# Pre-made weight sums for the second feed-forward of a two-block transformer kernel

## The reference

```python
def conv_ffn(x, w_up, conv_w, conv_b, w_down):      # w_up [1024, 5632], w_down [2816, 1024]
    h = x @ w_up
    h = causal depthwise convolution of width 3 over tokens, per column of h, + conv_b
    a, g = jnp.split(h, 2, axis=-1)
    return (jax.nn.silu(g) * a) @ w_down
```

## Time and profile before

| | before |
|---|---|
| median of 3 runs | 3193.47 us (3189.94 to 3194.23) |
| span of the profiled execution | 3197.4 us, 3.9 us above the median |
| PE busy | 3000.9 us, 94% |
| DVE, ACT, POOL busy | 1954.1, 1224.8, 606.6 us |
| loop of E, from first to last product | 1245.2 to 1657 us |
| loop of H, from first to last product | 2484.3 to 2929 us |

### The profile page before, as it was taken

How to read it: one execution, slowest core, us unless ns; L and a number is a source line. 1 busy time by engine, 2 the same in 40 slices (tenths; PEclk the granted TensorE clock), 3 DMA queues, 4 the chain that set the end, 5 groups by cost and what they waited for, 6 DMA issues and landing times.

```text
span 3197.4 us, 40840 instructions
## 1 busy us (share of the span) xinstructions
PE 3000.9 (94%) x15215; PEld 2446.6 (77%) x15215; DVE 1954.1 (61%) x2600; ACT 1224.8 (38%) x1900; POOL 606.6 (19%) x533
## 2 busy tenths in 40 slices
PE   8999999999989898999999988999888899999997
PEld 7777878878867677888878877888777677777886
DVE  3555565674674547555556674555646777776667
ACT  3531541531632445333322133565734443333212
POOL 3210110210221301322210000333411222221000
PEclk8999999999989899999999999999989999999999
DMA  4232212212222542222232244343334122223233
GB/s 138 69 94 59 89 60 67 94 54 73 82 80 77 213 145 86 79 79 79 79 113 105 93 131 123 86 135 122 120 106 146 53 79 79 79 72 105 93 105 119
DMA packets 227118, 308.16 MB, mean 96 GB/s; under 512 B 12162, under 2 KB 175248, under 8 KB 224416
## 3 DMA queue, kind: packets, MB, share of 16 engines
q1 hardware_dynamic: 207648, 244.93, 24.1%
q0 software_dynamic: 13520, 44.48, 4.1%
q10 hardware_dynamic: 5808, 16.79, 1.9%
HBM read 223.26 MB, written 82.90 MB: 96 GB/s over the span
## 4 chain that ended last, share of the span: by engine, by line
PE 66%; issue 12%; DVE 9%; ACT 4%; DMA 4%; POOL 4%; SPq 0%; POOLq 0%; ACTq 0%; DVEq 0%
PE PS L658 20%; PE PS L364 19%; PE PS L2314 13%; PE PS L1442 2%; PE PS L1408 1%; PE PS L1336 1%; POOL down_raw L1979 1%; POOL down_raw L1982 1%; PE PS L1325 1%; PE PS L2919 1%; DMA sb_branch<-u_scratch 1%; POOL down_raw L1977 1%; PE PS L2906 1%; DVE hL L439 1%; PE PS L1501 1%
## 5 line engine op out<-in xcount | busy, mean ns | idle before, releaser
L658 PE MATMUL PS<-hH,w_H 128*128 128x512 f32 x1072 | 455.8, 425 | 28.2 <-DVE w_L L321 15.3
L658 PE MATMUL PS<-hH,w_L 128*128 128x512 f32 x1072 | 428.2, 399 | 0.0
L658 PE MATMUL PS<-hL,w_H 128*128 128x512 f32 x1072 | 425.9, 397 | 0.0
L2133 DVE TENSOR_TENSOR ffn_sum<-ffn_sum,PS 128x1024 f32<-128x1024 f32 x160 | 195.4, 1221 | 139.4 <-PE PS L364 139.4
L321 DVE TENSOR_TENSOR w_L<-w_raw,w_H 128x1024 fp32r<-128x1024 f32 x107 | 133.6, 1251 | 217.4 <-ACT w_H L316 217.4
L658 PEld LDWEIGHTS PS<-hH,w_H 128*128 128x128 f32 x1072 | 208.0, 194 | 74.0 <-issue 16.0
L658 PEld LDWEIGHTS PS<-hH,w_L 128*128 128x128 f32 x1072 | 205.8, 192 | 46.8
L2314 PE MATMUL PS<-hH,fast_w 128*128 128x512 f32 x672 | 227.2, 399 | 10.3 <-ACT gate_up L2068 7.6
L658 PEld LDWEIGHTS PS<-hL,w_H 128*128 128x128 f32 x1072 | 207.7, 194 | 35.9 <-issue 1.7
L2212 DVE TENSOR_TENSOR gate_up<-PS,gate_up 128x512 f32<-128x512 f32 x210 | 144.1, 686 | 133.8 <-PE PS L2314 128.7
L2314 PE MATMUL PS<-sums,w_H 128*128 128x512 f32 x672 | 213.9, 400 | 9.3 <-DVE gate_up L2212 8.8
(11 more groups left out here) (459 smaller groups left out, 6569.1 us busy)
## 6 DMA issues: line engine op xcount, KB each, us to landing
w_raw<-in_w_in SPq DMA_DIRECT2D x62, 512.0 KB, 4.4
u_scratch<-unit_staged SPq DMA_DIRECT2D x50, 512.5 KB, 4.9
w_raw<-in_w_up SPq DMA_DIRECT2D x44, 512.0 KB, 4.2
hidden_scratch<-hidden SPq DMA_DIRECT2D x42, 512.0 KB, 3.0
gate_up<-hidden_scratch SPq DMA_DIRECT2D x20, 1024.0 KB, 4.9
w_raw<-in_w_ffn_gate SPq DMA_DIRECT2D x22, 512.0 KB, 3.9
w_raw<-in_w_ffn_up SPq DMA_DIRECT2D x22, 512.0 KB, 5.2
u_scratch<-unit_staged_f SPq DMA_DIRECT2D x21, 512.0 KB, 4.3
```

The costliest lines, as they stand in the source:

```text
L658: mm = e.matmul(PS[:, f.bank(o, half), :], w[:, k0 + k, :], x[:, k, half * HALF:(half + 1) * HALF], start=(k == 0 and j == 0), stop=(k == ...
L2133: e.tensor_tensor(yacc[:, b, :], yacc[:, b, :], bank2(4 + 2 * (b % 2)), ALU.add).then_inc(added, 1)
```

## The change

The four weight sums of H are no longer made tile by tile on GpSimd. All of T1 to T4, for all tiles, is made once in DRAM, in two tensors `up2_sums` of [1024 x 2816] float32, by 32 DMAs that GpSimd issues in stage B: 16 plain copies and 16 that add to their destination. Each moves 128 rows of 2816 numbers (1.44 MB), and each but the first waits for the completion of the one before. They are issued 2 + 4 + 4 in each of the first three pairs and 2 in the last. In H, SP loads for each tile the gate tile (512 KB), the half of the up tile that is still used raw (256 KB) and both sum tiles (512 KB each). GpSimd has nothing to do in H's loop. A DMA can add but not subtract, so all sums T become additions, and the signs move to the token sums and to `tile_sum`; E keeps GpSimd's sums, as additions. P6 goes to a PSUM bank of its own (3). In both E and H, tile 1's load moves behind the wait for the end of the stage before (`ffn_memory_free`).

```diff
+        up2_sums = [nc.dram_tensor(f"up2_sums{i}", [D, DFF], F32, kind="Internal").ap() for i in range(2)]
-            e.tensor_tensor(s1, s1, x2, ALU.add).then_inc(s, 1)
+            e.tensor_tensor(s1, s1, x2, ALU.subtract).then_inc(s, 1)
...
+        def up2_sum_parts(e):
+            w = a["w_up_2"][0]
+            gate, up = w[:, DFF:2 * DFF], w[:, 0:DFF]
+            top, low = slice(0, HALF), slice(HALF, D)
+            steps = [((0, top), gate[top], False), ((1, top), up[top], False),
+                     ((0, top), up[top], True), ((1, top), up[low], True),
+                     ((0, low), (0, top), False), ((0, low), up[low], True),
+                     ((1, low), (0, low), False), ((1, low), gate[low], True)]
+            n = 0
+            for (i, rows), src, add in steps:
+                dst = up2_sums[i][rows]
+                src = up2_sums[src[0]][src[1]] if isinstance(src, tuple) else src
+                for part in range(4):
+                    blk = slice(part * P, (part + 1) * P)
+                    if n:
+                        e.wait_ge(sem("up2_summed"), 16 * n)
+                    e.dma_start(dst[blk], src[blk], accum_op=ALU.add if add else ALU.bypass,
+                                max_dma_last_dim=2 * DFF)\
+                        .then_inc(sem("up2_summed"), 16)
+                    n += 1
+                    yield
...
         def pool_B(e):
+            parts = up2_sum_parts(e)
             for p in range(NPAIR):
...
                 if p == LAST:
                     o_low(range(4))
+                else:
+                    sums(2)
                 e.wait_ge(sem("rw_prepared"), at(PREP_OF["all"], p, 6))
...
                     e.memset(t[:, :, :], 0.0).then_inc(sem("inverse_zeroed"), 1)
+                sums(2 if p == LAST else 4)
                 for q in range(4):
...
+                sums(4)
                 e.wait_ge(sem("o_rw_written"), p + 1)
                 e.dma_start(o_scr[p + NPAIR], o_rw[:, :]).then_inc(sem("o_rw_stored"), 16)
...
-        Q_BANK, Q_FIRST = (0, 1, 0, 1, 2, 1, 2), (0, 1, 4)
+        Q_BANK, Q_FIRST = (0, 1, 0, 1, 2, 3, 2), (0, 1, 4, 5)
...
+            def weights(j, it=None):
+                e.dma_start(rg[:, :, :], tile(w_first, c_first, j, it)).then_inc(sem("fast_loaded"), 16)
+                if not summed:
+                    e.dma_start(ru[:, :, :], tile(w_second, c_second, j, it)).then_inc(sem("fast_loaded"), 16)
+                    return
+                e.dma_start(ru[:, 4:8, :], tile(w_second, c_second, j, it)[:, 4:8, :]).then_inc(sem("fast_loaded"), 16)
+                for i in range(2):
+                    e.dma_start(t_pair(i), tile(up2_sums[i].rearrange("(k p) c -> p k c", p=P), 0, j, it))\
+                        .then_inc(sem("fast_T"), 16)
...
+            if summed:
+                e.wait_ge(sem("up2_summed"), 16 * UP2_PARTS)
             ffn_memory_free(e, prev)
+            weights(1)
...
             def weight_sums(c, it):
+                if tag == "H":
+                    return
-                e.tensor_tensor(t_of(1), ru[:, 0:4, :], rg[:, 0:4, :], ALU.subtract).then_inc(sem("fast_T"), 1)
+                e.tensor_tensor(t_of(1), ru[:, 0:4, :], rg[:, 0:4, :], ALU.add).then_inc(sem("fast_T"), 1)
...
-                if Q_T[q]:
+                if Q_T[q] and tag == "H":
+                    e.wait_ge(sem("fast_T"), own("fast_T", tag, 32 * c + 32, it, 32))
+                elif Q_T[q]:
...
-                tile_sum(it, 4, uq[:, hi], 1, gq[:, hi])
+                tile_sum(it, 4, gq[:, hi], 1, gq[:, hi], "from", 1)
...
-                    if q >= 5:
-                        e.wait_ge(sem("fast_sum"), own("fast_sum", tag, q - 3, it, 5))
+                    if q == 5 and not first:
+                        e.wait_ge(sem("fast_sum"), own("fast_sum", tag, -1, it, 5))
+                    if q == 6:
+                        e.wait_ge(sem("fast_sum"), own("fast_sum", tag, 3, it, 5))
```

More of the change, by code:

```diff
@@ L18 @@
+import itertools
 from contextlib import ExitStack
@@ L208, in build @@
         SHARED["token_sums"] = {"D": 16, "G": 16}
+        SHARED["fast_T"] = {"E": 4 * NW, "H": 32 * NW}
         SHARED["masks_written"] = {"B": 1, "F": 0}
@@ L746, in pool_masks, with sums @@
             assert ch.n == N_MASK_STEPS, ch.n
+        UP2_PARTS = 32
+        def up2_sum_parts(e):
[19 more added lines that the diff above has]
+                    yield
         def pool_B(e):
+            parts = up2_sum_parts(e)
             for p in range(NPAIR):
+                def sums(n):
+                    for _ in itertools.islice(parts, n):
+                        pass
                 def weigh(s):
@@ L1920, in sp_ffn @@
             load_unit(e, U0 + 1, tile(w_second, c_second, 0))
-            for i, (w, col) in enumerate(((w_first, c_first), (w_second, c_second))):
+            rg, ru = raw[U0 % 2], raw[(U0 + 1) % 2]
+            summed = tag == "H"
+            def weights(j, it=None):
[7 more added lines that the diff above has]
+                        .then_inc(sem("fast_T"), 16)
+            for i in range(2):
                 e.wait_ge(s_wH, U0 + 1 + i)
                 e.wait_ge(s_wL, U0 + 1 + i)
-                e.sem_inc(s_held, 1)
-                e.dma_start(raw[(U0 + i) % 2][:, :, :], tile(w, col, 1)).then_inc(sem("fast_loaded"), 16)
+            if summed:
+                e.wait_ge(sem("up2_summed"), 16 * UP2_PARTS)
             ffn_memory_free(e, prev)
+            weights(1)
             e.dma_start(down_first[:, :, :], w_down[:, 0:2, :]).then_inc(sem("down_loaded"), 16)
@@ L1939, in turn @@
                     e.sem_inc(s_held, 1)
-                    for i, (w, col) in enumerate(((w_first, c_first), (w_second, c_second))):
-                        e.dma_start(raw[(U0 + i) % 2][:, :, :], tile(w, col, 2, it)).then_inc(sem("fast_loaded"), 16)
+                    weights(2, it)
                 else:
@@ L1988, in turn @@
                     weight_sums(1, it)
-            ffn_tiles(e, turn)
+            if tag != "H":
+                ffn_tiles(e, turn)
             e.wait_ge(sem("fast_P"), since(tag, "fast_P", 7 * NW))
@@ L2206, in tile_hidden, with tile_sum @@
                 e.tensor_tensor(hfE[:, :], hfE[:, :] if conv else uq, siE[:, :], ALU.mult).then_inc(hid, 1)
-            def tile_sum(it, p, out, bank, other, before=None):
+            def tile_sum(it, p, out, bank, other, op, before=None):
                 e.wait_ge(sem("fast_P"), own("fast_P", tag, p, it, 7))
@@ L2211, in tile_sum @@
                     e.wait_ge(sem("fast_sum"), own("fast_sum", tag, before, it, 5))
-                e.tensor_tensor(out, PS[:, bank, :], other, ALU.add).then_inc(sem("fast_sum"), 1)
+                x, y = (other, PS[:, bank, :]) if op == "from" else (PS[:, bank, :], other)
+                e.tensor_tensor(out, x, y, ALU.add if op == "add" else ALU.subtract).then_inc(sem("fast_sum"), 1)
             def turn(it, following):
@@ L2230, in turn @@
                 e.wait_ge(sem("fast_taken"), own("fast_taken", tag, 1, it, 2))
-                tile_sum(it, 2, uq[:, lo], 1, gq[:, hi])
+                tile_sum(it, 2, uq[:, lo], 1, gq[:, hi], "from")
                 if first:
@@ L2242, in turn @@
                     low(2, 1, it)
-                tile_sum(it, 5, uq[:, hi], 2, uq[:, hi], 2)
+                tile_sum(it, 5, uq[:, hi], 2, gq[:, hi], "sub", 2)
                 if following:
@@ L2246, in turn @@
                     low(4, 1, it)
-                tile_sum(it, 6, gq[:, hi], 1, gq[:, hi], 2)
+                tile_sum(it, 6, gq[:, hi], 3, gq[:, hi], "add", 3)
                 if conv:
@@ L2255, in turn @@
                     hidden_low(0, 1)
-                tile_sum(it, 7, uq[:, lo], 2, uq[:, lo], 1)
+                tile_sum(it, 7, uq[:, lo], 2, uq[:, lo], "sub", 1)
             ffn_tiles(e, turn)
@@ L2297, in turn @@
                     if q == 1 and not first:
-                        e.wait_ge(sem("fast_sum"), own("fast_sum", tag, -1, it, 5))
+                        e.wait_ge(sem("fast_sum"), own("fast_sum", tag, -3, it, 5))
                     if q == 2:
```

19 lines of the change are left out of this document (10 added, 9 removed).

## The result

The changed kernel takes 3178.01 us (median of 20 runs), the kernel before 3194.65 us (20 runs). The ratio is 0.9949, 95% interval 0.9939 to 0.9958, so 16.3 us less, give or take 3. The prediction was 3177, and its sum -16.5. The profiled execution has a span of 3175.2 us. That is 22.2 us less than the span before, but each span is that of one execution; the gain is read from the medians.

What follows compares the result with a forecast made beforehand. The prediction took H to be bound by a dependence loop through VectorE and q = 3, E by PE. H -22.0, E's start +2.5, B's DMAs +3.0 give -16.5: 3193.5 to 3177 us; likeliest 3170 to 3184, range 3166 to 3197.

Steps and rivals of the forecast that it cites:

- H's loop, -19.0: H's steady turns: period falls from 20.94 to 19.94 us without GpSimd's sums, 1.00 us in each of 19 turns.
- 9.63 + 11.31 = 20.94: H's old turn: q = 3 to `tile_sum` 6, 9.63 us, and back to q = 3, 11.31, set the period.
- Rival (4): H: VectorE's part shortens too, down to PE's 19.5 us, another 8.5 us, E's start hidden: 3165 to 3169; chance 0.08.
- I take 8.1 us: H's loop: time from issue to landing of a turn's loads, estimated at 7.9 to 8.6 us.
- deadline of 9.1: H's loop: loads must land within 9.1 us of issue (12.96 - 3.8), or `tile_sum` 6 is late.
- The spare "1.0 us": H's loop: margin between the loads' landing at 8.1 us and the 9.1 allowed; each us beyond costs 19.
- rival (1): H's loads land late, at 9.6 to 10.5 us, losing 10 to 27 us: 3187 to 3204; chance 0.15.
- H's start, -3.0: H's first turn: 3.0 us gained, 1.0 of it from VectorE steps no longer beside GpSimd's first sums.
- E's start, +2.5: E's start: tile 1's later load puts GpSimd's sums beside VectorE's lows, net loss 2.5 us, bounds -1 and +4.
- full blocking (3.5 to 4.5): E's start: VectorE's instructions blocked until GpSimd's end, alternating, a loss of 3.5 to 4.5 us.
- B's DMAs, +3: Stage B: the first two DMAs share the engines with loads ScalarE waits for, +3 us, bounds 0 and +12.
- the 12 us from rows: Stage B: time taken for one adding DMA of 1.44 MB, from trace rows of other transfers; a copy 8.

Runs made afterwards that it cites:

- signs_sum7: Kernel without B's DMAs, GpSimd's sums beside both loops, own bank and signs kept, plus H's `tile_sum` 7 ahead of low 5: 3196.16 us, 0.9999 of the kernel before.
- the closer of the two comparisons: Kernel with GpSimd's sums beside both loops, with B's 32 DMAs (result unused) against without: 3200.46 us against 3198.13, 5 us more, give or take 7.

## Why the prediction was right, and where it was not

**H's loop, -19.0.** Right in size: 19 turns from the first load's issue are 19.3 us shorter (mean period 20.96 before, 19.94 now), and the waits, the lows and the one stall left at q = 3 are as described. The step "9.63 + 11.31 = 20.94", by which the loop through q = 3 set the old period, was wrong. The loop through the loads set it, and the loop through q = 3 had 1.0 us to spare. Taking GpSimd away shortened the load loop by 1.55 us (12.10 to 10.55), 1.42 of it in VectorE's low 1 and 2; the sums themselves come no sooner (8.8 us after the issue, by GpSimd or by DMA). That alone would allow a period of 19.4. The loop through q = 3 now stops it at 19.97: from `tile_sum` 6 at 2684.50 to `tile_sum` 2 at 2695.08 it has the 10.6 us of the earlier trace rows, with the 0.74 to q = 3 11.3, and 8.65 from q = 3 at 2675.85 back. The prediction had that second loop right, from the last turn, and so the number. That the first loop would shorten by more than the second allows was luck, since the prediction didn't know that the first one bound. It would have been wrong about any edit that shortens only one of the two, as my expectation from it was about signs_sum7. Rival (4), PE's own period, came only with `tile_sum` 7 moved (19.34 to 19.38).

**The landing, "I take 8.1 us".** Mis-sized: 8.82, up to 9.41. The deadline of 9.1 was mis-sized the same way: it is 9.42, since q = 3 comes 4.44 us after the issue in place of 4.33 and `high` 1 to `tile_sum` 6 takes 3.67 in place of 3.8. The spare "1.0 us" is 0.6 on average and nothing in the worst turn, so rival (1) was near. Its price holds: a landing later by 1.73 us made the period 1.16 longer, which is the delay less the spare 0.6. (SP issues two loads more a turn, not four; they do take it 2 us.)

**H's start, -3.0.** `tile_sum` 6 of the first turn starts 39.6 us after SP's free memory before and 37.0 now: -2.6. It is held by the landing, as described; the landing came 0.8 us later than taken. From the free memory to the last product H takes 438.2 us where it took 460.1: -21.9 in all, against -22.0.

**E's start, +2.5.** +2.2 up to tile 2's load, in the profile of every kernel, and by the way described: sums beside lows. VectorE's loss of 4.0 us is what the prediction had for full blocking (3.5 to 4.5), and an idle time that it didn't count hides 0.8. What the clock takes in E comes on top in most profiles. The times can't tell either from 0.

**B's DMAs, +3.** Two copies cost about 5 us where they lie, for the reason given (the load for which ScalarE waits there lands 4.4 us later), the others nothing that shows. Over the whole program the cost lies between -2 and +12 us by the closer of the two comparisons. The times taken were 8 us for a copy and 12 for an addition. From issue to landing the 16 copies take 6.0 to 11.9 (median 6.6) and the 16 additions 9.9 to 15.2 (median 11.7).

The prediction's estimate from the Trainium skill (Collectives: The Full Stack, section "The bandwidth ceiling") was 5.8 us and the fixed part for an addition. The quickest addition here takes 9.9 us, so the measurement is above it, and the 12 us from rows was the better value.

**The sum.** -21.9 + 2.2 + (-2 to 12) = -22 to -8, with -16.3 measured. Read backwards, the measured gain leaves 3 us, give or take 3, for B and for what the clock takes in E. What stays open is how these two share it.

## What to carry to other kernels

Where two loops of dependences run through a turn, find the one that binds by a quantity that varies from turn to turn: here the period was the landing of the loads plus a constant 12.10 us. A path that adds up to the period is no proof, since both loops do when they share instructions. Before sums are made ahead of time to free an engine, look at which other engine's instructions run beside them; here it was those that became shorter, and the sums came no earlier.

## What the runs showed of the hardware

- A copy of 1.44 MB from DRAM to DRAM that GpSimd issues lands in 6.0 to 11.9 us (median of 16: 6.6), one that adds to its destination in 9.9 to 15.2 us (median of 16: 11.7). The slowest copies are the two that run beside other loads, and the load of that stretch for which ScalarE waits takes 10.0 us in place of 5.6.
- The same code gets another granted clock from one kernel to the next. From 710 to 720 us it is 0.58 in one and 1.00 in another, after 10 us in which PE was busy for 8.3 us in both. In E it falls to 1.2 GHz behind a pause of PE of 3.0 to 3.4 us in ten kernels of twelve. From tile 2's load to the last product E takes 404.2 to 404.4 us where the clock stays, 405.6 to 407.3 where it falls: 1.2 to 3 us, as much as the small terms of this case.
- VectorE's subtraction of 128x512 takes 0.69 us alone and 1.54 and 1.79 beside GpSimd additions of 1.3 to 1.6 us, even when nothing waits for those.
